# Order of the second projections' tiles, shape of the last out-projection's tiles, and the place of two loads

## Chip, cores, metric

One core of one Trainium2 chip runs the whole program in one launch. The metric is the device time of that launch in microseconds (us); smaller is better.

## What is computed

Two layers of a diffusion backbone over 1024 latent tokens (a grid of 16 rows and 64 columns) and 256 context tokens, width 1024, float32. Layer 0 is gated attention over all tokens. Layer 1, which the change touches, is neighbourhood attention: every latent query sees 8 x 16 grid neighbours and the 256 context tokens.

```
h, hc  = rms_norm(x, norm_g) * (1 + scale) + shift        # latent, context
q, k, v, g = split(h @ w_in, 4)                           # 1024 columns each, 16 heads of 64
kc, vc     = the same of hc (no q and no gate for the context)
s_loc = q . k_window * 64**-0.5 + rpb[...]                # 8 x 16 neighbours
s_ctx = q . kc * 64**-0.5
p     = softmax([s_loc, s_ctx])
o     = p_loc . v_window + p_ctx . vc
x     = x + gate * ((o * silu(g)) @ w_out)
return rms_norm(x, final_g)
```

Every matrix product is made of three: both factors are split into a high part (rounded to the short float format of TensorE) and the rest, and high x high, high x low and low x high are added.

## The kernel before

The program is five blocks in a row; a block ends when all engines are done with it. The last two matter here.

**Second projections** (`out_and_second_projections`, from 883 to 1323 us). After layer 0's out-projection, 24 tiles of 128 output columns are computed, in the order 8 tiles of q, 8 of k, 8 of g (gate), and after them v in 40 small tiles. A tile of q or g is two chunks of 512 tokens, one of k has a third chunk of 256 context tokens. `tile(n)` on TensorE (L1486 to L1488) does 24 matmuls a chunk. Weights come in pairs of tiles: `weights(pair)` on the SP queue (L1342) loads 1 MB into a single buffer `raw`. ScalarE casts one half (`high(n)`, L1572), VectorE subtracts (`low2(n)`, L1674). Results leave PSUM by `out(n)` on ScalarE (L1582 q, L1590 and L1593 k, L1600 g with SiLU) and, for q and k only, by `out_low(n)` on VectorE (L1690, L1694, L1699), which writes the low part. SP then stores them to DRAM scratch with `store(n, j)`: 8 DMAs of 256 KB for a tile of q (L1374, L1377), 12 for a tile of k (4 of 64 KB and 8 of 256 KB), 1 of 512 KB for one of g (L1361). The staging buffer has 3 slots.

Three orders set the pace. On SP, in a loop over n, the load for pair n/2+1 is issued ahead of the stores of tile n when n is even, and so behind all the stores of tile n-1; the loads of v's weights (L1352) stand after the stores of tiles 2, 3 and 16. On ScalarE and VectorE, in a loop over n, the cast for tile n stands ahead of the eviction of tile n-2:

```
for n in range(2, NT + 2):        # ScalarE; VectorE has the same with low2, v_low, out_low
    if n < NT: high(n)            # waits for the load of pair n // 2
    if n in (KT, KT + 2): v_high((n - KT) // 2)
    out(n - 2)
```

On TensorE tile n waits for the low part of its weights and for the eviction of tile n-2, whose banks it takes. After tile 23 `last_weights` (L1396) waits for all stores and issues 8 loads of 512 KB; v's stores stand behind it on SP.

**Neighbourhood attention and out-projection** (`neighbourhood_and_out`, from 1328 us to the end). The grid is cut into 4 strips of 16 columns. A unit is a strip and a pair of heads; 32 units, each of 4 steps (2 heads x 2 halves of 8 rows). SP loads for each unit, in this order: `kq_in` 1 MB (L1839), `bias_in` twice, 384 KB each (L1832), `vg_in` four DMAs of 128 KB (L1846), one of 256 KB (L1848) and the gate, 128 KB (L1851). All have two or three buffers; `vg_in(u)` waits for the products of unit u-2, and `kq_in(u+1)` stands behind it. In the first strip each unit also loads 256 KB of context keys (L1855). The final gain (512 KB, L1861) is loaded behind unit 1's loads.

GpSimd multiplies the heads' result by the gate (L2082, L2087) and splits it into `ohi` and `olo` (L2093, L2095), 256 tokens of a strip at a time. 36 steps behind the scores, `o_step(p)` gives TensorE one of the 16 pieces of an out-projection tile of 128 tokens (`out_project`, L1926 to L1928): tile 2s+f is half f of strip s, which is 8 rows of 16 columns. Per tile, `x_in(tile)` (ScalarE's queue, L1979) loads the residual `x_strip`, VectorE adds (`residual`, L2041), ScalarE takes the norm (L1973, L1975), VectorE scales (`finish`, L2047), and `x_out(tile)` (ScalarE's queue, L1983) stores 512 KB; `x_in(tile + 1)` stands right behind it. There is one `x_strip` buffer. `tile_rows` gives the DRAM side of both transfers:

```
s, f = tile // 2, tile % 2
return ap.rearrange("(r w) d -> r w d", w=GRID_W)[8 * f:8 * f + 8, STRIP_W * s:STRIP_W * (s + 1), :]
```

`x_in(0)` is issued ahead of ScalarE's loop, at the start of the block. For steps 128 to 163 there is no attention left, only the out-projection of the last tiles.

Of the kernel before, what the change touches and what calls it, by code (L numbers as in the profile page):

```python
# [15 lines left out]
ALU = mybir.AluOpType  # L16
# [1177 lines left out]
def out_and_second_projections(c, io, consts, mod, qk, hi, lo, wa, w1, w_out, w, w_out1):  # L1194
# [35 lines left out]
    with c.scope():  # L1230
# [39 lines left out]

        def lanes(n):
            chunks = ALL_CHUNKS if KT <= n < 2 * KT else LAT_CHUNKS
# [10 lines left out]

        def item(n, j=0):

            return n + 2 * max(0, min(n - KT, KT)) + j

        ITEMS = item(NT)

        def stored_by(i):  # L1290

            return sum(128 if o < item(KT) else 64 if o < item(2 * KT) else 16 for o in range(i % 3, i, 3))

        def evicted(eng, n):

            if n < 2 * KT:
                eng.wait_ge(outl, item(n + 1))
            else:
                eng.wait_ge(outg, n - 2 * KT + 1)
# [11 lines left out]

        def v_stored_by(u):

            return sum(16 if o % TT < CT else 32 for o in range(u % 3, u, 3))

        with c.block() as block:
            @block.sync
            def _(sp):
# [36 lines left out]
                def store(n, j=0):  # L1355

                    i = item(n, j)
                    slot = i % 3
                    if n >= 2 * KT:
                        sp.wait_ge(outg, n - 2 * KT + 1)  # L1360
                        sp.dma_start(io["gl"][n - 2 * KT, :, :], gstage[:, slot, 0:NLAT]).then_inc(stored[slot], 16)  # L1361
                        return
                    sp.wait_ge(outl, i + 1)
                    width = NCTX if n >= KT and j == 0 else NLAT
                    for low in range(2):
                        for a in range(2):
                            from_ = stage[64 * a:64 * a + 64, slot, low * NLAT:low * NLAT + width].bitcast(F32)
                            if KT <= n and j == 0:
                                to = io["kc"][n - KT, 64 * low:64 * low + 64, a, :]
                            else:  # L1370
                                at = 2 * STRIP_KEYS + 256 * a if n < KT else STRIP_KEYS * a + 256 * (j - 1)
                                to = io["kq"][n % KT, :, 64 * low:64 * low + 64, at:at + 256].rearrange("s p n -> p s n")
                                from_ = from_.rearrange("p (s n) -> p s n", s=STRIPS)
                            sp.dma_start(to, from_).then_inc(stored[slot], 16)  # L1374
                            if n < KT:
                                to = io["kq"][n, :, 64 * (1 - low):64 * (1 - low) + 64, at + 512:at + 768].rearrange("s p n -> p s n")
                                sp.dma_start(to, from_).then_inc(stored[slot], 16)  # L1377
# [46 lines left out]
            def _(pe):  # L1424
# [46 lines left out]
                def tile(n):  # L1471
# [10 lines left out]
                    if n == KT:  # L1482
                        pe.wait_ge(lod, N)
# [35 lines left out]
            def _(act):  # L1519
# [54 lines left out]
                def out(n):  # L1574
# [3 lines left out]
                    if n < KT:  # L1578
# [6 lines left out]
                    elif n < 2 * KT:  # L1585
# [42 lines left out]
            def _(dve):  # L1628
# [52 lines left out]
                def out_low(n):  # L1681
                    for j in range(3 if n >= KT else 1):
                        slot = item(n, j) % 3
                        dve.wait_ge(outh, item(n, j) + 1)
                        high_, low_ = stage[:, slot, 0:NLAT], stage[:, slot, NLAT:2 * NLAT]
                        bank, _, width = lanes(n)[j]
                        if n < KT:
# [14 lines left out]
                for n in range(2, NT + 2):  # L1702
# [4 lines left out]
                    if n - 2 < 2 * KT:  # L1707
                        out_low(n - 2)
# [43 lines left out]
def neighbourhood_and_out(c, io, consts, w_hi, w_lo):  # L1752
# [15 lines left out]
    with c.scope():  # L1768
# [55 lines left out]
        with c.block() as block:  # L1824
            @block.sync
            def _(sp):
# [26 lines left out]
                for u in range(UNITS):  # L1853
# [6 lines left out]
                    if u == 1:  # L1860
# [3 lines left out]
            def _(pe):  # L1864
# [54 lines left out]
                def out_project(tile, b, k):  # L1919
# [5 lines left out]
                    tok, cols = slice(f * P, (f + 1) * P), slice(512 * b, 512 * b + 512)  # L1925
                    pe.matmul(acc[:, b, :], ohi[:, s % 2, k, tok], w_hi[:, k, cols], start=(k == 0), stop=False)  # L1926
                    pe.matmul(acc[:, b, :], ohi[:, s % 2, k, tok], w_lo[:, k, cols], start=False, stop=False)  # L1927
                    last = pe.matmul(acc[:, b, :], olo[:, s % 2, k, tok], w_hi[:, k, cols], start=False, stop=(k == PAIRS - 1))  # L1928
# [16 lines left out]
            def _(act):  # L1945
# [126 lines left out]
            def _(pool):  # L2072
                for i in range(SETS + 1):
                    pool.memset(bias[:, i * (2 * LOCAL + NCTX):i * (2 * LOCAL + NCTX) + NCTX], 0.0).then_inc(zero, 1)
                for gr in range(STEPS // 2):
# [12 lines left out]
                    if a == 1:  # L2088
# [96 lines left out]
```

## Time and profile before

| | us |
|---|---|
| median of 3 runs (1802.07 to 1817.99) | 1803.52 |
| the profiled execution | 1799.4 |
| its span, from first to last instruction or transfer | 1797.6 |
| TensorE busy | 1623.1 (90%) |
| VectorE, ScalarE, GpSimd busy | 799.8, 782.8, 309.0 |
| chain that ended last: DMA | 7% of the span |

Times of rows are from the start of the span. PE is TensorE's matmuls, PEld its weight loads, DVE VectorE, ACT ScalarE, POOL GpSimd; SPq and ACTq are DMA issues on the queues of SP and ScalarE. "L1486" is a line of the kernel. A row of a timeline has start, duration, engine, line, operation and tiles; "[9.50 <-DVE ...]" is how long the engine stood idle before it and who ended that. Matmuls overlap, so that the duration of one is longer than its share of the engine's time.

### The profile page before, as it was taken

To read this page: it belongs to the slowest core of one execution; us is meant where nothing else is said; L and a number is where in the kernel's file an instruction comes from. 1 tells how busy PE (TensorE), PEld (TensorE's weight loads), DVE (VectorE), ACT (ScalarE), POOL (GpSimd) and SP (SyncE) were. 2 spreads that over 40 slices of the span, in tenths; PEclk is the share of its full clock that TensorE was granted. 3 is DMA by queue.
4 is the path that set the end of the run, shared out by engine and by line. 5 is a ranking of instruction groups with operands and counts; after the bars stand their busy time and mean duration, and the time that the engine had idled before them with its cause. 6 is when DMAs were issued, how large, how long until landed. Compare 5 with 4: busy or idle time off the path is not lost. (4 is left out here: it accounts for less than half of the span.)

```text
span 1797.6 us, 26314 instructions
## 1 busy us (share of the span) xinstructions
PE 1623.1 (90%) x9936; PEld 1396.4 (78%) x9936; DVE 799.8 (44%) x1866; ACT 782.8 (44%) x1802; POOL 309.0 (17%) x331
## 2 busy tenths in 40 slices
PE   7789999998999999899997899899958997788875
PEld 3167778897989999788775787789958997788774
DVE  1622211215888888644321323102117775566551
ACT  4221212215777777655511213211117775666561
POOL 0102110001222111100200000008103332232230
PEclk9889999999999999999998999999979998999898
DMA  7445411317111440142167666516369977777752
GB/s 286 135 154 177 139 47 50 117 68 216 41 21 22 156 156 16 56 125 81 59 181 216 173 202 186 188 71 188 94 166 295 281 257 201 227 211 205 217 144 59
DMA packets 190849, 264.56 MB, mean 147 GB/s; under 512 B 33554, under 2 KB 149860, under 8 KB 186596
## 3 DMA queue, kind: packets, MB, share of 16 engines
q1 hardware_dynamic: 188548, 254.49, 46.8%
q10 hardware_dynamic: 2176, 8.39, 1.9%
q8 instruction: 80, 1.31, 0.3%
q14 instruction: 45, 0.37, 0.1%
HBM read 193.62 MB, written 85.05 MB: 155 GB/s over the span
## 5 line engine op out<-in xcount | busy, mean ns | idle before, releaser
L1486 PE MATMUL p<-h_hi,w_hi 128*128 128x512 f32 (+1 forms) x448 | 171.9, 384 | 31.4 <-DVE p_stage L1690 11.4
L2016 DVE CUSTOM_DVE_ANT_0 nprob<-nS,bias_sets 128x640 f32<-128x640 f32 x128 | 105.4, 823 | 149.8 <-PE nS L1878 74.2
L1487 PE MATMUL p<-h_lo,w_hi 128*128 128x512 f32 (+1 forms) x448 | 170.4, 380 | 0.0
L1488 PE MATMUL p<-h_hi,w_lo 128*128 128x512 f32 (+1 forms) x448 | 170.3, 380 | 0.0
L600 PE MATMUL pp<-h_hi,w_hi 128*128 128x512 f32 (+1 forms) x432 | 157.4, 364 | 8.6 <-PEq L124 8.6
L1958 ACT CAST npt_hi<-nTB 128x256 fp32r<-128x256 f32 (+1 forms) x256 | 100.0, 426 | 128.1 <-PE nTB L1889 127.2
L601 PE MATMUL pp<-h_lo,w_hi 128*128 128x512 f32 (+1 forms) x432 | 154.2, 357 | 0.0
L602 PE MATMUL pp<-h_hi,w_lo 128*128 128x512 f32 (+1 forms) x432 | 154.1, 357 | 0.0
L1109 ACT ACTIVATE prob<-S,nm,qk_inv 128x512 f32<-128x512 f32 (+1 forms) x208 | 146.2, 706 | 8.7 <-DVE nm L1045 8.7
L1063 DVE TENSOR_TENSOR ptlo<-TB,pthi 128x512 fp32r<-128x512 f32 (+1 forms) x192 | 114.7, 598 | 29.7 <-ACT pthi L1121 27.9
L1121 ACT CAST pthi<-TB 128x512 fp32r<-128x512 f32 (+1 forms) x192 | 99.2, 517 | 63.1 <-PE TB L990 62.5
L1486 PEld LDWEIGHTS p<-h_hi,w_hi 128*128 128x128 f32 x448 | 86.7, 193 | 50.5 <-issue 32.4
L1038 DVE TENSOR_REDUCE mx<-S 128x1 f32<-128x512 f32 (+1 forms) x208 | 116.7, 580 | 16.7 <-PE S L982 15.4
L2029 DVE TENSOR_TENSOR npt_lo<-nTB,npt_hi 128x256 fp32r<-128x256 f32 (+1 forms) x256 | 114.6, 483 | 18.0 <-ACT npt_hi L1958 16.8
L1949 ACT ACTIVATE nprob<-nprob,nnm 128x640 f32<-128x640 f32 x128 | 107.0, 836 | 21.1 <-DVE nnm L2016 20.3
L1674 DVE TENSOR_TENSOR w_lo<-w_raw,w_hi 128x1024 fp32r<-128x1024 f32 x22 | 26.9, 1223 | 190.6 <-ACT w_hi L1572 190.6
L990 PE MATMUL TB<-ident,prob 128*128 128x128 f32 x672 | 108.7, 274 | 1.8 <-ACT prob L1109 0.9
L1877 PE MATMUL nS<-k_ctx,kq_strip 128*128 128x128 f32 (+1 forms) x192 | 50.9, 281 | 64.8 <-DMA kq_strip<-kq_scratch 54.0
L1572 ACT CAST w_hi<-w_raw 128x1024 fp32r<-128x1024 f32 x22 | 23.0, 1048 | 197.0 <-DMA w_raw<-in_na_w_in 156.8
L600 PEld LDWEIGHTS pp<-h_hi,w_hi 128*128 128x128 f32 x432 | 82.9, 192 | 32.9 <-issue 22.1
L1889 PE MATMUL nTB<-ident,nprob 128*128 128x128 f32 x640 | 99.2, 287 | 7.7 <-DVE npt_lo L2029 6.7
L667 ACT CAST w_hi<-w_raw 128x1024 fp32r<-128x1024 f32 x16 | 16.8, 1048 | 203.9 <-PE pp L602 180.0
(228 smaller groups left out, 4387.2 us busy)
## 6 DMA issues: line engine op xcount, KB each, us to landing
kq_scratch<-p_stage SPq DMA_DIRECT2D x128, 256.0 KB, 4.2
kq_strip<-kq_scratch SPq DMA_DIRECT2D x32, 1024.0 KB, 8.2
bias_sets<-bias_scratch SPq DMA_DIRECT2D x64, 384.0 KB, 8.1
v_strip<-v_scratch SPq DMA_DIRECT2D x128, 128.0 KB, 3.1
wmod<-in_mod_w SPq DMA_DIRECT2D x24, 512.0 KB, 4.6
wside<-in_mod_w SPq DMA_DIRECT2D x12, 1024.0 KB, 5.1
bias_scratch<-bias_wide_scratch SPq DMA_DIRECT2D x16, 768.0 KB, 11.0
w_raw<-in_na_w_in SPq DMA_DIRECT2D x11, 1024.0 KB, 7.8
```

Source lines behind the costliest of these rows:

```text
L600: pe.matmul(acc, whi[:, k, ws], hi[:, k, a:a + width], start=(k == 0), stop=False)
L601: pe.matmul(acc, whi[:, k, ws], lo[:, k, a:a + width], start=False, stop=False)
L602: last = pe.matmul(acc, wlo[:, k, ws], hi[:, k, a:a + width], start=False, stop=(k == KT - 1))
L990: last = pe.transpose(TB[:, no % 2, b * P:(b + 1) * P], prob[:, p % 5, a + b * P:a + (b + 1) * P], consts["ident"][:, :])
L1038: dve.tensor_reduce(mx[:, p % 5, k:k + 1], S[:, score_bank(p, k), 0:n], AX, ALU.max).then_inc(mxd, 1)
L1063: dve.tensor_tensor(lo[:, blocks, :], TB[:, no % 2, 0:n].rearrange("p (b q) -> p b q", q=P), hi[:, blocks, :], ALU.subtract).then_inc(lod, 1)
L1109: act.activation(prob[:, p % 5, a:a + n], S[:, score_bank(p, k), 0:n], ACT.Exp, bias=nm[:, p % 5:p % 5 + 1], scale=q_scale(h - 1, p) if p ...
L1486: pe.matmul(ps[:, bank, 0:width], whi[:, k, ws], hi[:, k, a:a + width], start=(k == 0), stop=False)
L1487: pe.matmul(ps[:, bank, 0:width], whi[:, k, ws], lo[:, k, a:a + width], start=False, stop=False)
L1488: last = pe.matmul(ps[:, bank, 0:width], wlo[:, k, ws], hi[:, k, a:a + width], start=False, stop=(k == KT - 1))
L1949: act.activation(pr, pr, ACT.Exp, scale=-1.0, bias=nm[:, p % 4:p % 4 + 1], accum_out=sums[:, p % 8:p % 8 + 1]).then_inc(expd, 1)
L2029: dve.tensor_tensor(ptlo[:, p // 2 % 2, to, :], TB[:, k, 0:n * P].rearrange("p (b q) -> p b q", q=P), pthi[:, p // 2 % 2, to, :], ALU.subt ...
```

## The change

Three parts. The q and g tiles of the second projections alternate in pairs (q0 q1 g0 g1 q2 q3 g2 g3 ...), and the k tiles come last; the rest of that part of the diff keeps counts of items, semaphores and stores right for a list of kinds. The last out-projection's tile is a column block of 8 columns and all 16 rows; GpSimd writes `ohi` and `olo` in that order of tokens. The load of the first residual is issued at step 16, and that of the final gain behind unit 4's loads.

```diff
+        SEQ = [(kind, i + x) for i in range(0, KT, 2) for kind in "qg" for x in range(2)] + [("k", i) for i in range(KT)]
+        K0 = SEQ.index(("k", 0))
...
         def columns(n):
-            return (n if n < 2 * KT else n + KT) * P
+            kind, i = SEQ[n]
+            return {"q": 0, "k": D, "g": 3 * D}[kind] + i * P
...
+        def parts(kind):
+            return 3 if kind == "k" else 1
+
         def item(n, j=0):
-            return n + 2 * max(0, min(n - KT, KT)) + j
+            return sum(parts(kind) for kind, _ in SEQ[:n]) + j
...
+        STORES = [16 * {"q": 8, "k": 4, "g": 1}[kind] for kind, _ in SEQ for _ in range(parts(kind))]
         def stored_by(i):
-            return sum(128 if o < item(KT) else 64 if o < item(2 * KT) else 16 for o in range(i % 3, i, 3))
+            return sum(STORES[o] for o in range(i % 3, i, 3))
...
                 for n in range(NT):
                     if n % 2 == 0 and n // 2 + 1 < NT // 2:
                         weights(n // 2 + 1)
-                    for j in range(3 if KT <= n < 2 * KT else 1):
+                    for j in range(parts(SEQ[n][0])):
                         store(n, j)
                     if n in (2, 3):
                         v_weights(n - 2)
-                    elif n == 2 * KT:
+                    elif n == K0:
                         v_weights(2)
                         v_weights(3)
...
-                    if n == KT:
+                    if n == K0:
                         pe.wait_ge(lod, N)
...
         def tile_rows(ap, tile):
-            s, f = tile // 2, tile % 2
-            return ap.rearrange("(r w) d -> r w d", w=GRID_W)[8 * f:8 * f + 8, STRIP_W * s:STRIP_W * (s + 1), :]
+            return ap.rearrange("(r w) d -> r w d", w=GRID_W)[:, 8 * tile:8 * tile + 8, :]
...
                     vg_in(u)
-                    if u == 1:
+                    if u == 4:
                         sp.dma_start(gain[:, :], io["final_g"].rearrange("(a d) -> a d", a=1).broadcast_to([P, D])).then_inc(gl, 16)
...
-                x_in(0)
                 for p in range(END):
                     q = p - LAG
+                    if p == 16:
+                        x_in(0)
...
-                        pool.tensor_copy(ohi[:, s % 2, i, :], o[:, :]).then_inc(ohd, 1)
+                        hi, lo = (o_[:, s % 2, i, :].rearrange("p (h r c) -> p r h c", h=2, c=8) for o_ in (ohi, olo))
+                        raw = o[:, :].rearrange("p (r h c) -> p r h c", h=2, c=8)
+                        pool.tensor_copy(hi, raw).then_inc(ohd, 1)
                         pool.wait_ge(ohd, u + 1)
-                        pool.tensor_tensor(olo[:, s % 2, i, :], o[:, :], ohi[:, s % 2, i, :], ALU.subtract).then_inc(old, 1)
+                        pool.tensor_tensor(lo, raw, hi, ALU.subtract).then_inc(old, 1)
```

## Rows read from the trace of the kernel before

**Rows 1.** Groups by line, 884 to 1207 us: busy, mean ns, idle before, releasers.
```profile
L1486 PE MATMUL p<-h_hi,w_hi 128*128 128x512 f32 (+1 forms) x448 | 171.9, 384 | 31.4 <-DVE p_stage L1690 11.4 <-DVE p_stage L1699 8.7 <-issue 5.4
```
**Rows 2.** Timeline of TensorE, second projections.
```profile
961.77 0.76 PE L1486 MATMUL p<-h_hi,w_hi 128*128 128x512 f32 x1 [9.50 <-DVE p_stage L1690]
```
**Rows 3.** Timeline of ScalarE, second projections.
```profile
957.74 1.04 ACT L1572 CAST w_hi<-w_raw 128x1024 fp32r<-128x1024 f32 x1 [27.27 <-DMA w_raw<-in_na_w_in]
...
1048.66 1.05 ACT L1572 CAST w_hi<-w_raw 128x1024 fp32r<-128x1024 f32 x1 [13.91 <-DMA w_raw<-in_na_w_in]
...
1078.18 1.05 ACT L1572 CAST w_hi<-w_raw 128x1024 fp32r<-128x1024 f32 x1 [13.52 <-DMA w_raw<-in_na_w_in]
...
1174.94 1.05 ACT L1572 CAST w_hi<-w_raw 128x1024 fp32r<-128x1024 f32 x1 [8.85 <-PE p L1488]
...
1185.82 1.05 ACT L1572 CAST w_hi<-w_raw 128x1024 fp32r<-128x1024 f32 x1 [8.85 <-PE p L1488]
```
**Rows 4.** Timeline of SP's queue, second projections.
```profile
930.11 0.58 SPq L1374 DMA_DIRECT2D kq_scratch<-p_stage  x1
...
947.82 2.09 SPq L1342 DMA_DIRECT2D w_raw<-in_na_w_in  x1
961.65 0.59 SPq L1374 DMA_DIRECT2D kq_scratch<-p_stage  x1
```
**Rows 5.** Timeline of TensorE, first strip of the last block.
```profile
1392.60 0.36 PE L1877 MATMUL nS<-k_ctx,kq_strip 128*128 128x256 f32 x1 [2.56 <-issue]
```
**Rows 6.** Windows, TensorE: busy, granted clock, DMA share, GB/s.
```profile
1394.00:1398.00 4.00, 4.00 (x23) 0.57 1.05 266
```
**Rows 7.** Timeline of SP's queue, second strip of the last block.
```profile
1475.69 1.71 SPq L1846 DMA_DIRECT2D v_strip<-v_scratch  x4
...
1488.43 1.93 SPq L1846 DMA_DIRECT2D v_strip<-v_scratch  x4
...
1494.76 0.43 SPq L1839 DMA_DIRECT2D kq_strip<-kq_scratch  x1
...
1500.43 1.71 SPq L1846 DMA_DIRECT2D v_strip<-v_scratch  x4
...
1521.40 1.71 SPq L1846 DMA_DIRECT2D v_strip<-v_scratch  x4
...
1532.49 1.71 SPq L1846 DMA_DIRECT2D v_strip<-v_scratch  x4
```
**Rows 8.** Timeline, all engines, the same place: ScalarE's queue.
```profile
1489.57 0.62 ACTq L1979 DMA_DIRECT2D x_strip<-x_scratch  x1
```
**Rows 9.** Tile kq_strip, SP, 1477 to 1480 us.
```profile
DMA to landing us min/median/max: 7.8/7.8/7.8
```
**Rows 10.** Tile kq_strip, SP, 1490 to 1496 us.
```profile
DMA to landing us min/median/max: 13.6/13.6/13.6
```
**Rows 11.** Waits of TensorE, 1495 to 1512 us: in total, times, longest.
```profile
PE nS L1877 <- DMA kq_strip<-kq_scratch: 7.2, 1, 7.2
```
**Rows 12.** The page, DMA queues: packets, MB, share of 16 engines over the span.
```profile
q10 hardware_dynamic: 2176, 8.39, 1.9%
```
**Rows 13.** The chain that ended last, in order of time.
```profile
1328.24 11.39 DMA kq_strip<-kq_scratch
...
1761.31 10.14 DMA x_strip<-x_scratch
```
**Rows 14.** Windows by stage, first strip: span, busy by engine, clock, DMA, GB/s.
```profile
1328.00:1424.00 96.00, 73.62 (x558) 70.33 (x559) 59.64 (x172) 61.72 (x154) 26.85 (x42) 0.87 0.95 286
```
**Rows 15.** Timeline of TensorE, tail.
```profile
1772.30 0.79 PE L1926 MATMUL nacc<-w_last_hi,on_hi 128*128 128x512 f32 x1 [5.82 <-DVE x_strip L2041]
```
**Rows 16.** Timeline, all engines, tail.
```profile
1791.14 0.62 ACTq L1983 DMA_DIRECT2D out<-x_work  x1
```
**Rows 17.** Tile x_scratch (its 8 stores on SP's queue, 512 KB each).
```profile
DMA to landing us min/median/max: 3.2/3.2/3.3
```
**Rows 18.** Line L2095: ns min/median/max, first and last start.
```profile
L2095 POOL TENSOR_TENSOR on_lo<-n_o,on_hi x32: 727/732/745, 1367.3 to 1758.2; 128x256 fp32r<-128x256 f32 x32
```

More of the change, by code:

```diff
@@ L1282, in v_buffers, with split_item, gates, v_stored_by @@
             return vw[i % 2]
+        def parts(kind):
+            return 3 if kind == "k" else 1
         def item(n, j=0):
-            return n + 2 * max(0, min(n - KT, KT)) + j
+            return sum(parts(kind) for kind, _ in SEQ[:n]) + j
+        def split_item(n, j=0):
+            return sum(parts(kind) for kind, _ in SEQ[:n] if kind != "g") + j
+        def gates(n):
+            return sum(kind == "g" for kind, _ in SEQ[:n])
         ITEMS = item(NT)
+        STORES = [16 * {"q": 8, "k": 4, "g": 1}[kind] for kind, _ in SEQ for _ in range(parts(kind))]
         def stored_by(i):
-            return sum(128 if o < item(KT) else 64 if o < item(2 * KT) else 16 for o in range(i % 3, i, 3))
+            return sum(STORES[o] for o in range(i % 3, i, 3))
         def evicted(eng, n):
-            if n < 2 * KT:
-                eng.wait_ge(outl, item(n + 1))
-            else:
-                eng.wait_ge(outg, n - 2 * KT + 1)
+            if SEQ[n][0] == "g":
+                eng.wait_ge(outg, gates(n + 1))
+            else:
+                eng.wait_ge(outl, split_item(n + 1))
+        def v_stored_by(u):
+            return sum(16 if o % TT < CT else 32 for o in range(u % 3, u, 3))
         def strips(ap):
@@ L1355, in store @@
                 def store(n, j=0):
[L1357 to L1361, printed above, removed]
+                    kind, m = SEQ[n]
+                    slot = item(n, j) % 3
+                    if kind == "g":
+                        sp.wait_ge(outg, gates(n + 1))
+                        sp.dma_start(io["gl"][m, :, :], gstage[:, slot, 0:NLAT]).then_inc(stored[slot], 16)
@@ L1362, in store @@
                         return
[L1363 to L1364 removed]
+                    sp.wait_ge(outl, split_item(n, j) + 1)
+                    width = NCTX if kind == "k" and j == 0 else NLAT
                     for low in range(2):
                         for a in range(2):
+                            rows, other = slice(64 * low, 64 * low + 64), slice(64 * (1 - low), 64 * (1 - low) + 64)
                             from_ = stage[64 * a:64 * a + 64, slot, low * NLAT:low * NLAT + width].bitcast(F32)
[L1368 to L1377, printed above, removed]
@@ new lines, in store @@
+                            if kind == "k" and j == 0:
+                                sp.dma_start(io["kc"][m, rows, a, :], from_).then_inc(stored[slot], 16)
+                                continue
+                            at = 2 * STRIP_KEYS + 256 * a if kind == "q" else STRIP_KEYS * a + 256 * (j - 1)
+                            from_ = from_.rearrange("p (s n) -> p s n", s=STRIPS)
+                            sp.dma_start(io["kq"][m, :, rows, at:at + 256].rearrange("s p n -> p s n"), from_).then_inc(stored[slot], 16)
@@ L1379, in v_store @@
+                            if kind == "q":
+                                sp.dma_start(io["kq"][m, :, other, at + 512:at + 768].rearrange("s p n -> p s n"),
+                                             from_).then_inc(stored[slot], 16)
                 def v_store(u):
@@ L1681, in out_low @@
                 def out_low(n):
-                    for j in range(3 if n >= KT else 1):
+                    kind = SEQ[n][0]
+                    if kind == "g":
+                        return
+                    for j in range(parts(kind)):
                         slot = item(n, j) % 3
-                        dve.wait_ge(outh, item(n, j) + 1)
+                        dve.wait_ge(outh, split_item(n, j) + 1)
                         high_, low_ = stage[:, slot, 0:NLAT], stage[:, slot, NLAT:2 * NLAT]
                         bank, _, width = lanes(n)[j]
-                        if n < KT:
+                        if kind == "q":
                             for f, (bank, _, _) in enumerate(lanes(n)):
@@ L1924, in out_project @@
                         pe.wait_ge(x2d, 2 * (tile - 1) + b + 1)
[L1925 to L1928, printed above, removed]
+                    cols = slice(512 * b, 512 * b + 512)
+                    h, l = (o_[:, s % 2, k, f * P:(f + 1) * P] for o_ in (ohi, olo))
+                    pe.matmul(acc[:, b, :], h, w_hi[:, k, cols], start=(k == 0), stop=False)
+                    pe.matmul(acc[:, b, :], h, w_lo[:, k, cols], start=False, stop=False)
+                    last = pe.matmul(acc[:, b, :], l, w_hi[:, k, cols], start=False, stop=(k == PAIRS - 1))
                     last.then_inc(om, 1)
```

12 lines of the change are left out of this document (5 added, 7 removed).

## Prediction, made before the changed kernel was run

> **What bounds the kernel now.** I read the page first: TensorE is busy 90% of the span, so what can be won is the idle tenth and the stretches at half clock. The groups by line and the timelines of the engines say where these lie. In the second projections TensorE sat idle 31.4 us before L1486 [rows 1]; 2.5 us of that stand before tile 0 and 28.9 between tiles. The longest, 9.5 us, ended with a q tile's eviction on VectorE [rows 2]. ScalarE shows what is behind it: its cast of the next weights waited 27.3 us for their load, up to 957.74 [rows 3], and the evictions stand behind the cast. SP's queue shows why the load is late: it issues the stores of two q tiles from 930.11 to 947.82, and only then the load, which lands at 957.74 [rows 3, 4]. So a closed loop sets the pace: two tiles' stores 17.7, landing 9.9, cast, eviction and first store 3.9 (957.74 to 961.65), 31.5 us a pair of q tiles [rows 3, 4]. TensorE needs 10.88 us for a tile with two chunks (the distance of the last two casts, which wait for TensorE) [rows 3], 21.8 for a pair. Key tiles have the same loop: 29.5 us a pair (1048.66 to 1078.18) [rows 3] against 2 x 10.88 x 1280/1024 = 27.2. Gate tiles have none, since one store is one issue.
>
> In the last block three places matter. In its first strip the DMA engines are busy 95% at 286 GB/s [rows 14], and the chain begins with an 11.4 us load [rows 13]. From the second strip on, a unit takes 11.09 us, the distance of SP's first issue for it from 1521.40 to 1532.49, but around each tile's end two units take longer: 12.0 and 20.97 us [rows 7]. There TensorE waited 7.2 us for a kq load [rows 11], which took 13.6 us where the one before took 7.8 [rows 9, 10]. What differs is that ScalarE issued `x_out` and `x_in` at that moment [rows 8]. In the tail, with attention over, each tile waits 10.1 us for its residual [rows 13].
>
> One row explains both: ScalarE's queue moved its 16 transfers of 128 rows of 4 KB as 2176 packets [rows 12]. That is 136 each: 128, and 8 more. If each engine that takes part adds one, these transfers ran on 8 engines of 16, with 16 rows on each.
>
> **Part 1, order of the projections.** No instruction is added or taken. Followed from 906 us, where the first two q tiles are done: g0 and g1 take TensorE to 928.4, while the stores of q1 and the load for q2 run as before. g0 must be evicted for q2, and ScalarE does it behind the cast at about 927: idle 1.3 us. v's first two weight loads (2 MB) now stand ahead of the load for g2 with only two gate stores before them, so that it lands about 947, and the stores of q2 and q3 start late, at 951. They end at 966, the load for q4 lands at 974.5, v's cast (twice the elements of one of 1.05 us [rows 3]) comes ahead of g2's eviction: idle about 5.4 us. The two later q pairs have nothing in the way. From the end of q4: q5's matmuls 10.9, eviction up to the first store 3.9, q5's stores 8.2 (17.7 for two with a load of v's weights among them), landing 8 (it was 9.9 with that load ahead), cast and subtraction 2.3, sum 33.3, where TensorE has three tiles left, 32.6. So idle 0.7, twice. The loop is as long as before, but 43.5 us of matmuls lie over it, no longer 21.8.
>
> The keys then start behind gates, so that the first key pair's successor has its weights in time. For the next pairs the loop of 29.5 against 27.2 us holds at most twice, and v's last two loads (2 MB) fall among key stores: I take 4 us, between 0 and the 9 that four key pairs would lose. At the end `last_weights` now waits for 12 stores a tile, where it waited for one; v's stores behind it start, as I estimate, 18 us after the last tile instead of 10. Cover: 6 PSUM banks and 3 staging slots let TensorE run 9 v tiles ahead (24 matmuls of 256 columns, a quarter of 10.88 us each), 24 us; I count 1 us for the third v tile's bank. The sum of idle is 1.3 + 5.4 + 1.4 + 4 + 1 = 13.1 us, against 28.9.
>
> Half clock comes on top. After 2.56 us of idling [rows 5] the granted clock was 0.57 for 4 us, the lower level (1.2 GHz) for most of them [rows 6]; that costs 4 x 0.43 = 1.7 us. Four stalls of that kind become two: 3.4 us back. Part 1: 15.8 + 3.4 = 19 us less. Bounds: 10 (the keys lose all they lost before and v's loads 5 more) and 30.
>
> **Part 2, tiles of 16 rows by 8 columns.** The same bytes, in 16 blocks of 8 rows of 4 KB. If the number of engines follows the outer dimension, it goes from 8 to 16, and each engine carries 8 rows a transfer. What a row costs: the last store is issued at 1791.14 [rows 16] and ends with the span at 1797.6, 5.8 us after its 0.6 of issue, with 16 rows an engine; store and load together take 0.7 + 10.14 [rows 13], with 32. So 0.31 us a row, and 0.8 fixed.
>
> The Trainium skill ("DMA: Bandwidth & Descriptors", section "Why a DMA increments its semaphore by 16 and not by 1") says that a DMA uses the largest number up to 16 that divides the slowest dimension on both sides. The 136 packets agree with it, and by it the change gives 16 engines; without it the 16 is an inference from one number. The same page ("Anatomy of one DMA — SWDGE (gpsimd) path") puts the fixed part at about 2.0 us. By that, halving would give back 1.9 us of the last store and not 2.5, and the sum would be 1 us smaller. The 512 KB stores of x_scratch, 128 rows from as many partitions, land in 3.2 us [rows 17], which is 0.8 + 8 x 0.31 and not 3.9.
>
> In the middle: 16 rows fewer per engine are 5 us less delay of the kq load. Before, it landed 19.9 us after the unit's first issue (1488.43 to 1494.76 + 13.6), where the unit before needed 2.7 + 7.8 = 10.5: 9.4 late, of which 7.2 became a stall [rows 7, 9 to 11], so 2.2 are free. Afterwards it is 4.4 late (at most 5): a stall of 2.2. The stretch loses (12.0 - 11.1) + (20.97 - 11.09) = 10.8 us now [rows 7], that is 7.2 and 3.6 at half clock. With 2.2 and the 1.7 from above it loses 3.9, so 6.9 less, in five places (the ends of tiles 0 to 4): 34 us. Bounds: 0, if the number of engines doesn't matter, and 54, if stall and clock go altogether. The table loads of ScalarE around the norm (12.7 us for the unit from 1475.69) [rows 7] stay.
>
> The tail: the load of tile 6's residual starts at 1761.31 and lands 5.1 us later, 1766.4 and not 1771.45. TensorE, which began tile 7 at 1772.30 after 5.8 us idle [rows 15], begins at 1767.3, without a fall of the clock, and takes 10.9: 1778.2. The last residual is in by 1776.7, so that TensorE is late next. A round of the tail is (1791.14 + 0.65 - 1761.31) / 2 = 15.2 us [rows 13, 16], 5.1 without the load; less one of its two adds and the store's issue, 3.8. The last store is issued at 1782.0, 9.1 earlier, and lands 2.5 sooner: 11.5 us less. Bounds 0 and 13.
>
> GpSimd's two copies get runs of 8 elements. They have 11 us a unit and are 36 steps ahead of their use: nothing. If the cover were gone: see rival E.
>
> **Part 3, two loads later.** `x_in(0)` and the gain, 1 MB, leave the opening and come back around 1370 to 1375, in the same strip, where the DMA engines are full [rows 14]. The first kq load (11.4 us [rows 13]) had 16 rows of the residual beside it on 8 engines; without them it lands 3 to 5 us sooner, and the gain gives another 1.6 (0.5 MB at 286 GB/s, 1.8). The return costs 1 MB at 286 GB/s, 3.7 us. Net 2 us less, between 5 less and 2 more. ScalarE's issue of 0.6 us at step 16 is in that.
>
> **Sum.** 19 + 34 + 11.5 + 2 = 66.5 us. The profiled execution took 1799.4 and would take 1733; the median of the runs is 4 higher, so 1737 there.
>
> **Rivals.**
> B. The transfers are not shorter with 16 engines. For it: in the middle's stall keys, bias and residual are all on their way, and it may be memory that is slow; kq loads that wait 13.6 us [rows 10] would then wait as long. Against it: rows 12 and 17. Then parts 1 and 3 alone: 1803.5 - 21 = 1782. Chance 0.10.
> C. The new order gives only half: the loop moves to the keys, whose tiles have 12 stores and 2 MB of v's weights among them. Part 1 is then 10: 1746. Chance 0.15.
> D. The middle's stalls go altogether, because x's packets start while the engines are idle between two units: 54 for 34, 1717. For it: the free 2.2 us. Chance 0.15.
> E. The other side, slower: GpSimd becomes the bound by its copies in runs of 8. Now the second is 0.73 us [rows 18] and the first shorter, all of GpSimd's work for a unit about 4 us, 2.9 of it other work. It decides from 11.1 - 2.9 = 8.2 us for the two on; to eat 66.5 us over 32 units it takes 2.1 more, 10.3 us, nine times the present. At 12 us a unit has 3.8 more, 122 in all: 1858. Against it: no row shows anything like it. Chance 0.03.
> My forecast: 0.57.
>
> **How the numbers follow.** The likeliest is 1737. Its own terms give 1715 to 1755; to leave out no more than 2 in 10 the range takes in D and C and stops short of B: 1708 to 1766. Faster by over 1% (18 us, about what a measurement of this kernel tells from no change) are the forecast, B, C and D: 0.95, the other 0.02 of their sum left for what I have not seen. Within 1%: 0.02. Slower: 0.03 (E).
>
> **What would show it.** ScalarE's queue with 2304 packets, not 2176. Waits for kq after the first strip of about 2 us each, not 7.2, and unit distances near 14 where 20.97 stands. Idle before L1486 of about 15 us, most of it before q4 and in the keys; the casts of q's successors waiting for TensorE. A tail in which the last add waits for a matmul. x_in's landing near 5 us. If kq loads still take 13.6 us behind an `x_in`, part 2's reason is wrong; if TensorE stalls before every key tile, part 1's.

## The result, and the profile after

The changed kernel takes 1711.3 us (median of 4 runs, 1707.4 to 1713.3) against 1803.9 before; the ratio is 0.9468, with a 95% interval of 0.9417 to 0.9519. That is 96 us less than before (87 to 105) by the ratio, 93 by the two medians and 89 by the two profiled spans, where I had forecast 66.5. (One of the four runs of the kernel before took 1818.0 us, which pulls the ratio down.) Direction and places were right, the size was a quarter to a third too small; by the ratio the time, 0.9468 x 1803.5 = 1707.6, falls just below the lower edge of the range (1708).

From the page of the changed kernel: span, TensorE, ScalarE's DMA queue and the first matmul of the projections.

```profile
span 1708.5 us, 26314 instructions
PE 1601.2 (94%) x9936; PEld 1381.2 (81%) x9936; DVE 800.2 (47%) x1866; ACT 783.3 (46%) x1802; POOL 310.3 (18%) x331
...
q10 hardware_dynamic: 2304, 8.39, 1.9%
...
L1501 PE MATMUL p<-h_hi,w_hi 128*128 128x512 f32 (+1 forms) x448 | 168.2, 376 | 7.7 <-ACT g_stage L1616 3.8
```

The same matmuls idle 7.7 us in front, where it was 31.4 [rows 1]; 2.5 of them stand before tile 0. And 2304 packets for 16 transfers are 144 each, 128 and 16 more, where it was 128 and 8 [rows 12].

I cut both spans at the same events: first matmul of the projections, first matmul of v, first kq load, kq load of unit 11, issue of tile 6's residual, end.

| stretch | before | after | difference | forecast |
|---|---|---|---|---|
| up to the projections | 883.6 | 881.2 | -2.4 | 0 |
| 24 tiles of the projections | 324.5 | 292.7 | -31.8 | -19 with v |
| v tiles, to the last block | 120.1 | 127.6 | +7.5 | (in it) |
| units 0 to 11 | 116.9 | 111.3 | -5.6 | -2 |
| from there to tile 6's residual | 316.2 | 269.7 | -46.5 | -34 |
| tail | 36.3 | 25.9 | -10.4 | -11.5 |

**Projections.** Timeline of TensorE, changed kernel: the waits between tiles of the projections and among v's (in brackets the idle time in front, and what ended it).

```profile
927.19 0.47 PE L1501 MATMUL p<-h_hi,w_hi 128*128 128x512 f32 x1 [1.27 <-ACT g_stage L1616]
...
973.45 0.47 PE L1501 MATMUL p<-h_hi,w_hi 128*128 128x512 f32 x1 [2.49 <-ACT g_stage L1616]
...
1017.68 0.50 PE L1501 MATMUL p<-h_hi,w_hi 128*128 128x512 f32 x1 [0.43 <-DVE w_lo L1690]
...
1145.43 0.35 PE L1501 MATMUL p<-h_hi,w_hi 128*128 128x256 f32 x1 [1.06 <-DVE p_stage L1718]
...
1204.68 0.58 PE L1528 MATMUL p<-wv_hi,h_hi 128*128 128x256 f32 x1 [4.68 <-DVE v_stage L1733]
```

The first is g0's eviction behind the cast, 1.27 us (1.3 forecast). The second is q4 (2.5, not 5.4). The third is q6, the fourth a key tile. The four make 5.2 us, and the granted clock stayed at 1.00 in the 4 us behind each. Only one of the waits belongs to the keys, 1.06 us in 8 tiles. ScalarE's casts for g2, g4 and q6 show why q4 was early, and the pace after it:

```profile
941.70 1.05 ACT L1587 CAST w_hi<-w_raw 128x1024 fp32r<-128x1024 f32 x1 [12.73 <-DMA w_raw<-in_na_w_in]
...
984.71 1.05 ACT L1587 CAST w_hi<-w_raw 128x1024 fp32r<-128x1024 f32 x1 [9.48 <-PE p L1503]
...
1015.32 1.05 ACT L1587 CAST w_hi<-w_raw 128x1024 fp32r<-128x1024 f32 x1 [17.70 <-DMA w_raw<-in_na_w_in]
```

The load for g2, issued at 929.9, was there at 941.7 (I had counted 947, all of v's 2 MB ahead of it). At 984.71 the cast for g4, which follows a q pair, waits for TensorE; in the kernel before, the cast behind a q pair waited for its load (27.27 us) [rows 3]. The waits for loads aren't gone: the cast for q6 waited 17.70 us for one, up to 1015.32. But with a gate pair's matmuls over the loop it costs TensorE only 0.43 us.

The 324.5 us of the old order are not a fixed number. Three more runs have the old projections as they were: 324.3 (tile shape alone), 330.2 (the two loads alone) and 330.5 us (`x_in` later). Their idle time between tiles is about the same, 28.6 to 30.2 us; what differs is the granted clock, 0.97 in the kernel before and 0.96, 0.95 and 0.94 in these. So the new order gives 32 to 38 us, by how often the clock falls in the old one.

The fifth wait, 4.68 us, is new. ScalarE's and SP's timelines at v's first tiles, changed kernel:

```profile
1182.76 0.37 ACT L1640 CAST v_stage<-p 128x256 fp32r<-128x256 f32 x1 [2.51 <-PE p L1530]
1203.79 0.37 ACT L1640 CAST v_stage<-p 128x256 fp32r<-128x256 f32 x1 [20.66 <-DMA v_ctx_scratch<-v_stage]
```
```profile
1187.70 3.79 SPq L1411 DMA_DIRECT2D w_last_raw<-in_na_w_out  x8
1191.54 0.97 SPq L1399 DMA_DIRECT2D v_ctx_scratch<-v_stage  x2
```

SP could issue the last weights' 4 MB only at 1187.7, after the keys' stores, and v's first store at 1191.5, behind them. That store was not done until 1203.8, so that ScalarE had no staging slot for 20.7 us, and TensorE ran out of banks at v's tenth tile. In the 4 us behind that wait the granted clock was 0.50.

**Middle.** SP's queue, changed kernel, at the end of a tile: first issue of the unit, its kq issue, and the next two units.

```profile
1504.74 1.74 SPq L1864 DMA_DIRECT2D v_strip<-v_scratch  x4
...
1508.80 0.43 SPq L1857 DMA_DIRECT2D kq_strip<-kq_scratch  x1
...
1516.76 2.58 SPq L1864 DMA_DIRECT2D v_strip<-v_scratch  x4
...
1527.85 1.71 SPq L1864 DMA_DIRECT2D v_strip<-v_scratch  x4
```

The units take 12.0 and 11.1 us where [rows 7] had 12.0 and 21.0. The kq load takes 8.0 us, and not 13.6 as in [rows 10]:

```profile
DMA to landing us min/median/max: 8.0/8.0/8.0
```

It lands 4.1 + 8.0 = 12.1 us after the unit's first issue; of the units with no such transfer beside them the one before needed 10.7, the one before that 10.2. Against 10.2 it is 1.9 us late, inside the 2.2 that are free. This is the mildest of the five places: they are 3.5, 1.9, 2.0, 2.2 and 2.5 us late, 2.4 in the mean, and the kernel before has 9.4 to 10.1 at its five, counted from 10.5. From 1450 to 1690 TensorE waited once for kq, behind the load that was 3.5 us late:

```profile
PE nS L1895 <- DMA kq_strip<-kq_scratch: 1.0, 1, 1.0
```

**Opening and tail.** The wait before the first scores is 10.1 us, and was 16.2. In the tail x_in takes 5.9 us for 10.1 [rows 13], and TensorE waits 1.5 for 5.8 [rows 15]; the last store's issue and the span's end are 4.3 us apart, where it was 6.5 [rows 16]. TensorE's timeline (opening, then tail), the chain and ScalarE's queue:

```profile
1306.94 0.55 PE L1895 MATMUL nS<-k_ctx,kq_strip 128*128 128x256 f32 x1 [10.11 <-DMA kq_strip<-kq_scratch]
...
1689.30 0.50 PE L1945 MATMUL nacc<-w_last_hi,on_hi 128*128 128x512 f32 x1 [1.51 <-DVE x_strip L2061]
```
```profile
1682.56 5.90 DMA x_strip<-x_scratch
```
```profile
1704.25 0.57 ACTq L2002 DMA_DIRECT2D out<-x_work  x1
```

GpSimd's copies take what they took: the second has a median of 734 ns, and had 732 [rows 18]. Rival E had nothing to it.

### The profile page after: what moved, and what is told of

Same layout as the page of the kernel before. It is cut to its first block and busy times, and to the rows that moved or that the text cites. A ratio compares the mean times of both kernels' runs of the same rounds, so it can differ in the third digit from the quotient of the medians.

```text
span 1708.5 us, 26314 instructions
## 1 busy us (share of the span) xinstructions
PE 1601.2 (94%) x9936; PEld 1381.2 (81%) x9936; DVE 800.2 (47%) x1866; ACT 783.3 (46%) x1802; POOL 310.3 (18%) x331
## 3 DMA queue, kind: packets, MB, share of 16 engines
q10 hardware_dynamic: 2304, 8.39, 1.9%
## 5 line engine op out<-in xcount | busy, mean ns | idle before, releaser
L1501 PE MATMUL p<-h_hi,w_hi 128*128 128x512 f32 (+1 forms) x448 | 168.2, 376 | 7.7 <-ACT g_stage L1616 3.8
L1932 PE MATMUL nO<-npt_hi,v_strip 128*128 128x256 f32 (+1 forms) x384 | 103.0, 299 | 0.0
```

Source lines behind the costliest of these rows:

```text
L1501: pe.matmul(ps[:, bank, 0:width], whi[:, k, ws], hi[:, k, a:a + width], start=(k == 0), stop=False)
```

## Experiments

All are compared with the kernel before, run on the same chip between them. Times are medians. Where a run is set against the changed kernel, the two were measured in different sessions, and the ratios and the stretches of the traces are safer than the difference of medians.

### The parts one by one

**Order alone** (the changed kernel with the old tiles and the old places of both loads).

> Only the order of the second projections is new; tiles of the last out-projection and the two loads are as before. Theory (three parts that add up, by the stretches of the two traces): the projections are 32 us shorter, the v tiles behind them 7.5 us longer because v's first stores wait for the keys' stores and queue behind the loads of the last weights; together 24 us less than before, about 1779. Rival (the parts work through each other: the order also changed what the last block finds): the last block is not 470 us as before but clearly shorter, and the time is under 1770.

1778.9 us, ratio 0.9864 (0.9844 to 0.9884), 24.5 less. Projections 292.3 us, v 126.0, last block 471.1: as the changed kernel up to the last block, as the kernel before in it. The theory holds, the rival falls.

**Tile shape alone** (the kernel before with the new `tile_rows` and the token order in `ohi` and `olo`).

> Only the last out-projection's tiles are 16 rows of 8 columns. Theory (the transfers of ScalarE's queue go over 16 engines and not 8; that ends the stalls of the middle, 46 us, and shortens the tail, 10 us): 56 us less, about 1747, with 2304 packets on that queue and unit distances near 47 for a strip's half and not 56.8. My recorded term was 34 + 11.5. Rival (half of what the middle gained came from the loads that were moved or from a later start): 35 to 45 us less.

1737.9 us, ratio 0.9641 (0.9626 to 0.9655), 64.7 less, with 2304 packets. Its last block is 410.4 us against 469.4: 59 less. So the shape gives all of the middle and the tail by itself, and more than my 45.5.

**The two loads alone.**

```diff
-                    if u == 1:
+                    if u == 4:
                         sp.dma_start(gain...
-                x_in(0)
                 for p in range(END):
+                    if p == 16:
+                        x_in(0)
```

> Only the two loads are later. Theory (the opening's first kq load no longer shares engines with the residual): 2 to 6 us less, the wait before the first scores near 11 us and not 16; all of it in the first strip. Rival (what leaves the opening comes back in the same full strip): within 1 us of before.

1801.7 us, ratio 0.9991 (0.9975 to 1.0007): nothing. SP's queue in this run, the bias loads of unit 6:

```profile
1386.39 12.11 SPq L1832 DMA_DIRECT2D bias_sets<-bias_scratch  x2
```

The opening has what was expected (units 1 and 2 are 9.8 us apart and were 16.2), and a few units later it is gone: `x_in(0)`, issued at 1372, runs on 8 engines in a full strip, and units 6 and 7 are 20.6 us apart. The rival holds here. In the changed kernel the same load runs on 16 engines, and its largest distance in that place is 13.6. By the stretches it keeps some 4 us there: units 0 to 11 take 111.3 us with it and 115.2 with the shape alone. But that stretch varies by more between runs (109.5 to 118.1 in the six versions with all three parts), so that I can't call it shown.

### Is it the number of engines?

**Outer dimension 8 again, tile unchanged.** The 128 rows are the same, the partitions go by column and row.

```diff
-            return ap.rearrange("(r w) d -> r w d", w=GRID_W)[:, 8 * tile:8 * tile + 8, :]
+            return ap.rearrange("(r w) d -> w r d", w=GRID_W)[8 * tile:8 * tile + 8, :, :]
...
-     rearrange("p (h r c) -> p r h c", h=2, c=8)
+     rearrange("p (h c r) -> p r h c", h=2, c=8)
```

> The changed kernel with the same column blocks, the same 128 rows of 4 KB per transfer, but with partitions in the order column, row: the outer dimension of the DRAM side is 8 again, not 16 (GpSimd writes the tokens in that order; the result is the same). Theory (the outer dimension sets how many engines carry a transfer): 2176 packets again, x_in near 10 us in the tail, waits of 7 us for kq at each tile's end, and 1711 + 56 = 1767. Rival (the gain came from where the rows lie in memory or from the block's shape): 1711 as in the changed kernel, x_in near 6 us.

1775.2 us, ratio 0.9845 (0.9827 to 0.9863): 64 more than the changed kernel. The page's queue, TensorE's waits over the span, and the chain:

```profile
q10 hardware_dynamic: 2176, 8.39, 1.9%
```
```profile
PE nS L1895 <- DMA kq_strip<-kq_scratch: 50.1, 7, 9.9
```
```profile
1738.23 10.08 DMA x_strip<-x_scratch
```

The same rows of memory, in another order, bring back 2176 packets, the waits and the 10.1 us. The outer dimension of the DRAM side sets the number of engines, as the Trainium skill says ("DMA: Bandwidth & Descriptors", section "Why a DMA increments its semaphore by 16 and not by 1"); the block's shape and place have no part in it. Nor is it whether a row's neighbour in memory comes next: in the kernel before 16 in a row do, in this run each next row lies 64 rows further, and both are slow. That there are 8 or 16 engines is read from the packets; the profile doesn't list the engines of a transfer.

**How much it takes.** Two runs vary what one engine has to carry. In the kernel before, the load is issued two steps behind the store:

```diff
                     if done and done[1] == 1 and done[2] == PAIRS - 1:
                         x_out(done[0])
-                        if done[0] + 1 < TILES:
-                            x_in(done[0] + 1)
+                    done = o_step(p - 6)
+                    if done and done[1] == 1 and done[2] == PAIRS - 1 and done[0] + 1 < TILES:
+                        x_in(done[0] + 1)
```

> The kernel before, 8 engines for each transfer of ScalarE's queue, but x_in is issued two steps (5.5 us) behind x_out and no longer right behind it. Bytes and engines are as before. Theory A (what makes the keys' load late is how many rows an engine has in front of it when SP issues a unit's loads; 32 in a row choke SP's queue, 16 nearly fit the gap): the wait of 7.2 us at each tile's end falls to 0 to 3 us, unit distances add up to some 48 to 51 us a tile and not 56.8, 25 to 40 us less in all. Theory B (all bytes that those 8 engines must move until the load lands count, whenever they are issued): the stall only moves, within 10 us of before.

1797.3 us, ratio 0.9966 (0.9938 to 0.9994): theory B. The waits for kq from 1490 to 1780 us, in all, times, longest:

```profile
PE nS L1877 <- DMA kq_strip<-kq_scratch: 32.1, 5, 9.3
```

In the kernel before, the same stretch has 36.6 us in 5 waits. SP is less held up (kq is issued 5.1 us after the unit's first issue, not 6.3), but the load then takes 13.2 us beside an `x_in` on the same 8 engines. So what those engines have to move until the load lands counts more than when it was queued, at least for this one delay.

In the changed kernel, one more store a tile:

```diff
                     act.dma_start(tile_rows(io["out"][0], tile), work[:, :]).then_inc(st, 16)
+                    act.dma_start(tile_rows(io["again"], tile), work[:, :]).then_inc(st, 16)
```

> The changed kernel with one more store of 512 KB per tile (the same rows again, to a scratch tensor), right behind the first: 24 rows an engine at each tile's end, where the changed kernel has 16 and the kernel before 32. Theory A (a fixed 0.3 us per row on top of a free 2.2 us, as my prediction had it, with the measured start: the keys' load is 1.9 us late at 16 rows, so 4.4 at 24): waits of 2 us a tile and some 4 us of stall and half clock, 20 us more in the middle, 5 in the tail: 1736. Theory B (a threshold: below some 20 rows nothing, above it SP's queue blocks and the delay grows faster): 5 us and more of waiting a tile, 40 us or more in the middle, over 1755. Theory C (still free at 24): only the tail, 1716.

1725.3 us, ratio 0.9576 (0.9551 to 0.9601), 14 more than the changed kernel by medians, 17 by the spans. Waits of TensorE, 1450 to 1700 us, and SP's queue at the end of a tile:

```profile
PE nS L1895 <- DMA kq_strip<-kq_scratch: 4.7, 5, 1.6
```
```profile
1557.62 3.53 SPq L1864 DMA_DIRECT2D v_strip<-v_scratch  x4
...
1563.57 0.43 SPq L1857 DMA_DIRECT2D kq_strip<-kq_scratch  x1
```

The load lands 6.0 + 8.0 = 14.0 us after the unit's first issue, 3.8 late (3.8 to 4.5 at the five places). TensorE waits 0.9 us in a place, 5 us over the middle (from unit 11 to 31: 241.5 and 236.8), without a fall of the clock that would show there (0.99), and from unit 31 to the end the run takes 6.3 more. No theory has it all: the time lies between C's 1716 and A's 1736; in the middle, 5 us more is nearest to C's nothing, and A's 20 and B's 40 are out. With the other rows: 16 rows an engine are 1.9 us late at the place shown (2.4 in the mean), 24 are 3.8 (4.0), both on all engines, and 32 on half of them are 9.4.

### The loop in the projections

**The eviction ahead of the cast, in the old order.**

```diff
                 for n in range(2, NT + 2):
+                    out(n - 2)
                     if n < NT:
                         high(n)
                     if n in (KT, KT + 2):
                         v_high((n - KT) // 2)
-                    out(n - 2)
```
(and the same on VectorE)

> The kernel before, with one thing turned: on ScalarE and VectorE the eviction of tile n-2 stands ahead of the cast of the weights for tile n. Theory A (a closed loop: stores behind eviction, load behind stores, eviction behind the cast that waits for the load): without its last link the q pairs cost TensorE 1 to 3 us each and not 9, so 15 to 25 us less, 1779 to 1789. Theory B (the DMA engines or SP's queue are simply full with q's stores, 17.7 us of issues and 4 MB a pair): within 5 us of before.

1769.4 us, ratio 0.9806 (0.9764 to 0.9848), 32.5 less: more than theory A's 25, and more than the new order alone (24.5). The projections take 291.0 us, v 120.1. Windows of TensorE in this run: stretch, length, busy time and matmuls, granted clock, DMA share, GB/s:

```profile
882.60:1173.60 291.00, 288.73 (x1361) 0.99 0.63 190
```

Granted clock 0.99 and DMA at 190 GB/s over the stretch, against 170 in the kernel before: the same transfers went through in 33.5 us less, so neither the DMA engines nor SP's queue had been the limit. The wait was a loop, and its link was the order of two instructions on ScalarE (and of the same two on VectorE).

**Keys behind the first two q tiles** (`SEQ[:2] + keys + SEQ[2:]`; the loads of v's last weights stay behind tile 16).

> The changed kernel, with the 8 key tiles behind the first two q tiles and not at the end; q and gates still alternate, v's last two weight loads stay at tile 16. Theory A (what the alternation gives is that a q pair's stores have a gate pair's matmuls to hide under; keys last only matters for what comes behind them): the v stretch is 7 us shorter than in the changed kernel, and the key stretch loses 5 to 10 us, since its first pair stands behind q's stores: 1705 to 1717. Theory B (keys last is itself half of the gain): over 1720.

1726.3 us, ratio 0.9568 (0.9535 to 0.9601): theory B by its number, 15 more than the changed kernel by medians (17 by the spans). TensorE's timeline, this run:

```profile
962.40 0.55 PE L1502 MATMUL p<-h_hi,w_hi 128*128 128x256 f32 x1 [5.59 <-DVE p_stage L1719]
...
994.46 0.36 PE L1502 MATMUL p<-h_hi,w_hi 128*128 128x256 f32 x1 [2.80 <-DVE p_stage L1719]
...
1026.79 0.47 PE L1502 MATMUL p<-h_hi,w_hi 128*128 128x512 f32 x1 [4.55 <-DVE p_stage L1719]
...
1055.14 0.77 PE L1502 MATMUL p<-h_hi,w_hi 128*128 128x512 f32 x1 [4.68 <-ACT g_stage L1617]
```

v is 7.5 us shorter (120.1), as A said, but the projections take 312.0: the third and the fourth key pair wait 5.6 and 2.8 us, the first gate behind the keys 4.6, and the q tile behind the first gate pair 4.7 for a gate's eviction. Keys at the end have gates before them, whose loads are early, and behind them no tile that needs a load; that this is why they wait so little is my reading of the two traces.

The clock does not go by the length of the wait alone. In the 4 us behind the waits of 5.6, 4.6 and 4.7 us it was 0.54, 0.57 and 0.50, but behind the 2.80 us at 994.46 it stayed at 1.00 (first row; the columns are as above, with the busy time of all engines). In the run before this one it was 0.64 behind a wait of 2.00 us (second row):

```profile
994.46:998.46 4.00, 4.00 (x29) 3.83 (x30) 1.41 (x2) 0.37 (x1) 0.00 (x0) 1.00 0.78 210
```
```profile
951.50:955.50 4.00, 3.98 (x11) 3.14 (x12) 2.68 (x9) 0.62 (x1) 0.00 (x0) 0.64 0.66 195
```

**v's first ten stores ahead of the last weights.**

```diff
-                last_weights()
                 for u in range(VB * TT):
+                    if u == TT:
+                        last_weights()
                     v_store(u)
```

> The changed kernel, with the 8 loads of the last weights issued behind the stores of v's first 10 tiles and no longer ahead of them. Theory (the v tiles take 7.5 us longer than before because v's first stores are issued late and then sit behind 4 MB of loads; TensorE runs out of PSUM banks): the idle of 4.7 us at v's tenth tile and the half clock behind it go, 6 to 8 us less, about 1704. Rival (the keys' own stores hold the engines, not the loads): at most 2 us less.

1705.3 us, ratio 0.9462 (0.9436 to 0.9488). By medians 6 less than the changed kernel, by the ratios 1, and the intervals overlap, so the total decides nothing; the trace decides for the stretch. v's tiles take 120.1 us and not 127.6, and ScalarE waits for a slot 5.7 us and not 20.7. (From unit 11 to tile 6's residual this run takes 274.4 us against 269.7, so that 4.7 of it are gone again in the total; why, no run shows.)

```profile
1188.27 0.37 ACT L1641 CAST v_stage<-p 128x256 fp32r<-128x256 f32 x1 [5.74 <-DMA v_ctx_scratch<-v_stage]
```

The edit takes away two things at once: v's first store is issued at 1184.1, 7.5 us sooner, as it no longer waits with the last weights for the keys' stores to land, and it is done 4.2 us later and not 12.3.

### Versions with more than the change

**Both edits together.**

> The changed kernel with both edits of the two runs before: evictions ahead of casts, and the last weights' loads behind v's first 10 stores. Theory A (closed loop): the remaining idle between tiles (5.2 us) mostly goes, and v's 7 us: about 1700. Theory B (queue full): no better than with v's stores first alone, about 1704, or worse by up to 3 us where the cast is now late for a gate pair.

1703.7 us, ratio 0.9451 (0.9425 to 0.9478). Projections 292.0, v 120.1: the eviction's place gives nothing more once the order has given it (292.7). B by the time.

**The old order, with all else** (evictions ahead of casts, new shape, later loads).

> The kernel before (q, then keys, then gates) with evictions ahead of casts, the new tile shape and the two later loads: all but the new order. Theory A (with the cast out of the loop, the order has nothing left to give): the projections take 291 us, the v tiles 120, the last block 407 to 411; 1702 to 1706, the same as the changed kernel with both edits (1703.7). Theory B (order and evictions each have a share of their own): 5 us or more above that.

1701.8 us, ratio 0.9441 (0.9418 to 0.9464); projections 287.9, v 120.1, last block 408.9. Theory A: the new order and the turned eviction remove the same wait, and the turned eviction does so without moving the keys' stores in front of v's.

**x_in ahead of x_out, on top of both edits.**

> The run with both edits (evictions ahead of casts, v's first stores ahead of the last weights) and x_in issued ahead of x_out. Theory: in the tail the residual lands some 3 us after its issue and not 5.9, TensorE's 1.5 us of idling before tile 7 go, from the last unit's load to the end 1.5 to 3 us less than 58.9; about 1702. Rival (the store, now behind the load, ends later than what was won): no difference or 0.6 us more at the end.

1699.8 us, ratio 0.9435 (0.9411 to 0.9460), the fastest median, 101 below the kernel before run beside it, though its interval overlaps the two above. From the last unit's kq load to the end it takes 56.9 us, 2.0 less than the run with both edits, as expected.

## Why the prediction was right and wrong

**Part 1** was forecast as 19 us and is 24.3. That they are near is partly luck: the 24 tiles alone gave 31.8 where my terms make 20, and v took 7.5 back where I had 1. The loop was read rightly: the order alone removes it, and so does the turned eviction. Three terms were off. q4's stall was 2.5 and not 5.4, since the load for g2 came 5 us sooner. The keys' "4 us, between 0 and the 9" is 1.1, and of "idle 0.7, twice" 0.43 came once. And with the stalls short, no half clock was left, where I had kept two falls; the stretch's clock is 1.00 in the row below, and my 6.8 us for the old falls were also too few: 324.5 us less 28.9 of idling is 295.6, and the same matmuls now take 292.7 less 5.2, 287.5, so 8.1 us were lost to the clock. Windows by stage, changed kernel (busy time of TensorE, its weight loads, VectorE, ScalarE and GpSimd, then granted clock, DMA share, GB/s):

```profile
881.20:1173.80 292.60, 287.35 (x1359) 240.45 (x1360) 70.23 (x156) 67.75 (x135) 7.18 (x4) 1.00 0.61 182
```

The step that failed in the other direction is "Cover: 6 PSUM banks and 3 staging slots". I had v's first store issued 18 us after the last tile, and it was (1173.8 to 1191.5). But I let it end when it was issued: it took until 1203.8, 12.3 us, behind the 4 MB of `last_weights`. That is 30 us in all, more than the 24 of cover (TensorE in fact went on for 26, to 1200.0). The run with v's stores first gives the stretch its 7.5 us back.

**Part 2** is what made the number wrong. "At most 5 us late, a stall of 2.2", with 1.7 of half clock, was to leave 3.9 of 10.8 us at each of five places; 1.5 are left: 46.5 us of the possible 54 were won, so 7.5 remain over the five places (0.9 a place is the unit of 12.0 us, which stands there before and after). The mis-sized term is the lateness with 16 rows: 4.4 forecast, 1.9 to 3.5 measured, 2.4 in the mean, and so a stall of 2.2 at every place, where TensorE waited 1.0 at one and nowhere else; with the stalls the falls of the clock were gone too (a mean of 1.00 from 1450 to 1660 us, where the kernel before has 0.93 from 1450 to 1761). I had scaled the old one by rows, 9.4 less 16 x 0.31. The doses say why that fails: with all engines at work 8 further rows cost 1.6 us in the mean (1.9 by the two places shown), about 0.2 a row, not 0.31, and the old 9.4 had one thing in it that doesn't scale with rows an engine: SP stood 3.3 us in one issue in the old kernel, so that kq was issued 6.3 us after the unit's first load; it is 4.1 now, and 2.7 with no transfer beside it. Rival D had this ("x's packets start while the engines are idle between two units"), and I gave it 0.15. What share idle gaps and SP's queue have in it, each by itself, I have not separated.

**The tail** was 10.4 for 11.5, and the size was off the other way: 1.1 us too much. I took 0.8 us fixed and 0.31 a row from two rows, and set aside the fixed 2.0 that the Trainium skill gives ("DMA: Bandwidth & Descriptors", section "Anatomy of one DMA — SWDGE (gpsimd) path"). The page gives it for the path of GpSimd, and these transfers are on ScalarE's queue, so it was never more than an estimate here. Measured: the last store 3.7 us behind its issue (3.3 by my fit, 3.9 as an estimate by the Trainium skill's 2.0), x_in 5.9 (5.1 by my fit, 5.7 by the other estimate: 10.1 less 16 rows of (10.8 - 2.0) / 32), so that its number came nearer. So the residual was 0.8 us later than forecast, and TensorE idled 1.5 us that I had at none.

**Part 3** was forecast as 2 less. Alone it is nothing that can be measured (ratio 0.9991, 0.9975 to 1.0007); with 16 engines some microseconds may be its own, within the scatter of the opening. The return that I priced as bytes over bandwidth, 3.7 us, costs a single stall of 9.1 us when the load is on 8 engines (TensorE's wait before 1391.76 in the run with the two loads alone).

**The rivals.** B is out (the number of engines decides, by the run with outer dimension 8). C is out. D came nearest: it named 54 us for the middle, I 34, and 46.5 were won, with the stalls all but gone; that its reason, the idle engines between two units, is the true one is not shown. E is out.

## What to carry to other kernels

Count the packets per transfer of a queue: here those over the number of rows were 8 with an outer dimension of 8 and 16 with one of 16, and told on how many engines it ran. A DRAM view whose outer dimension is 8 kept a 512 KB transfer on half of them; order the view so that 16 stands outside. When stores, loads and casts wait for each other in a ring, look for the one link that is only an order of instructions on an engine, here a cast that waits for a load ahead of an eviction that doesn't. And when a block of stores moves to the end of a stage, look at what stands behind it on the same queue, with its landing time and not its issue time.

## What I had not expected of the hardware

The order of rows inside one transfer, with the same bytes at the same places in memory, is worth 64 us of 1711. And two waits of TensorE of about the same length, 2.00 and 2.80 us, were followed once by a fall of the clock and once by none, and the longer one had none. And on half of the engines the two transfers of ScalarE's queue hurt a third one far beyond their share: the 1 MB load of the keys beside them took 13.4 to 14.9 us (the kernel before and the run with outer dimension 8), against some 7.5 without them and 8.0 to 9.4 beside the same bytes on 16 engines in the changed kernel; even 1.5 MB on 16 engines left it at 8.0 to 9.4.
